# First tile's four merges of a bidirectional delta-rule recurrence: two at a time on two pairs of PSUM banks, with the loads of one direction ordered ahead of the other's

## The reference, cut to what matters

```python
def chunk_gated_delta(q, k, v, g, beta, s0):
    # S_t = a_t (I - b_t k_t k_t^T) S_{t-1} + b_t k_t v_t^T, o_t = S_t^T q_t, in chunks
    a_low = where(strict, einsum('bhnid,bhnjd->bhnij', k * beta, k) * decay, 0)
    sol = triangular_solve(a_low + eye, rhs, lower=True, unit_diagonal=True)
    ...
    def step(S, inp):                      # one chunk after the other
        v_new = u_n - w_n @ S
        o_n = qd_n @ S + att_n @ v_new
        return S * gt_n + kt_n^T @ v_new, o_n
# run once forwards and once backwards over the tokens, 8 heads of 128
```

## Time and profile before

| | |
|---|---|
| three executions | 2710.94 us median, 2702.87 to 2714.01 us |
| the profiled execution | 2701.26 us, of which the span is 2699.5 us |
| mean granted clock of TensorE | 0.932 of full speed |
| TensorE busy | 2307.3 us, 85% of the span |
| VectorE, ScalarE, GpSimd busy | 1019.7, 589.6 and 249.5 us |
| the recurrence's first matmul and the end of its loop | 399.3 and 707.4 us |

### The profile page before, as it was taken

How to read it: one execution, slowest core, us unless ns; L and a number is a source line. 1 busy time by engine, 2 the same in 40 slices (tenths; PEclk the granted TensorE clock), 3 DMA queues, 4 the chain that set the end, 5 groups by cost and what they waited for, 6 DMA issues and landing times. The chain is left out here.

```text
span 2699.5 us, 29938 instructions
## 1 busy us (share of the span) xinstructions
PE 2307.3 (85%) x11804; PEld 1514.6 (56%) x11804; DVE 1019.7 (38%) x1782; ACT 589.6 (22%) x1229; POOL 249.5 (9%) x295
## 2 busy tenths in 40 slices
PE   4999987699785897888888888885998989799998
PEld 2877657589674333333333333333775767688775
DVE  3677526545745010101011010115744554563443
ACT  4442213244411000000000000002332421223311
POOL 4223326500110000000000000000000000000000
PEclk8999988599887999999999999997998999899999
DMA  6123636354410999999999999994220131221030
GB/s 218 58 86 121 215 110 180 82 148 118 152 69 24 417 417 417 417 416 416 417 417 418 417 418 418 416 416 161 90 78 31 32 117 63 100 94 63 32 133 31
DMA packets 209222, 569.87 MB, mean 211 GB/s; under 512 B 62584, under 2 KB 97377, under 8 KB 175713
## 3 DMA queue, kind: packets, MB, share of 16 engines
q1 hardware_dynamic: 202104, 559.45, 54.5%
q0 software_dynamic: 2496, 8.40, 1.0%
q10 hardware_dynamic: 4521, 0.64, 0.1%
HBM read 540.14 MB, written 28.31 MB: 211 GB/s over the span
## 5 line engine op out<-in xcount | busy, mean ns | idle before, releaser
L1897 PE MATMUL ps_gate_up<-expert_ring_early,one_expert_columns 128*64 128x512 f32 x512 | 252.0, 650 | 87.6 <-DMA expert_ring_early<-in_moe_w_up_dram 73.8
L1897 PE MATMUL ps_gate_up<-expert_ring,one_expert_columns 128*64 128x512 f32 x512 | 233.4, 610 | 47.1 <-DMA expert_ring<-in_moe_w_up_dram 47.0
L1964 DVE TENSOR_TENSOR hidden_tokens<-silu_gate,ps_gate_up 64x512 f32<-64x512 f32 x64 | 42.5, 690 | 609.6 <-ACT silu_gate L1943 609.1
L1898 PE MATMUL ps_gate_up<-expert_ring_early,one_expert_columns 128*64 128x512 f32 x512 | 252.8, 651 | 0.0
L1898 PE MATMUL ps_gate_up<-expert_ring,one_expert_columns 128*64 128x512 f32 x512 | 234.0, 611 | 0.0
L1877 PE MATMUL ps_down<-expert_ring,hidden_columns 128*64 128x512 f32 x512 | 226.6, 595 | 0.0
L1878 PE MATMUL ps_down<-expert_ring,hidden_columns 128*64 128x512 f32 x512 | 226.6, 595 | 0.0
L1897 PEld LDWEIGHTS ps_gate_up<-expert_ring_early,one_expert_columns 128*64 128x64 f32 x512 | 73.4, 149 | 249.0 <-issue 249.0
L1897 PEld LDWEIGHTS ps_gate_up<-expert_ring,one_expert_columns 128*64 128x64 f32 x512 | 69.9, 141 | 193.0 <-issue 193.0
L1877 PEld LDWEIGHTS ps_down<-expert_ring,hidden_columns 128*64 128x64 f32 x512 | 67.5, 137 | 130.1 <-issue 127.9
L846 DVE SCALAR_TENSOR_TENSOR conv_out<-conv_in,tap_columns,conv_out 128x770 f32<-128x770 f32 (+1 forms) x96 | 124.2, 1294 | 3.4
(11 more groups left out here) (506 smaller groups left out, 4625.9 us busy)
## 6 DMA issues: line engine op xcount, KB each, us to landing
expert_ring<-in_moe_w_down_dram SPq DMA_DIRECT2D x64, 2048.0 KB, 19.5
expert_ring_early<-in_moe_w_gate_dram SPq DMA_DIRECT2D x32, 2048.0 KB, 16.1
expert_ring_early<-in_moe_w_up_dram SPq DMA_DIRECT2D x32, 2048.0 KB, 20.6
expert_ring<-in_moe_w_gate_dram SPq DMA_DIRECT2D x32, 2048.0 KB, 22.5
expert_ring<-in_moe_w_up_dram SPq DMA_DIRECT2D x32, 2048.0 KB, 24.2
win_ring<-in_gdn_w_in_dram SPq DMA_DIRECT2D x16, 1024.0 KB, 7.9
late_mod_ring<-in_w_mod_dram SPq DMA_DIRECT2D x16, 1024.0 KB, 5.4
stream_raw<-in_w_in_even_dram SPq DMA_DIRECT2D x16, 1024.0 KB, 5.2
```

The source lines that it names most:

```text
L1897: mm(psA[LO, c], xe[:, e, k], gu[s0][:, j, cols], start=(k == 0), stop=(k == KC - 1))
L1898: last = mm(psA[HI, c], xe[:, e, k], gu[s1][:, j, cols], start=(k == 0), stop=(k == KC - 1))
L1964: nc.vector.tensor_tensor(hid[HI, c % 2], sg[HI, c % 2], psA[HI, c], ALU.mult).then_inc(hidden, 1)
```

## The change

Merges 1 and 3 get banks 4 and 5 as their pair, all others keep banks 6 and 7. Merges 0 and 1 are interleaved step by step, then merges 2 and 3, all ahead of the loop, on TensorE and on ScalarE. On VectorE `merged(0)` and `merged(1)` stand behind rows 16 and 17, `merged(2)` and `merged(3)` behind rows 26 and 27. `product32(1)` waits for all decays (the last readers of banks 4 and 5), `product32(2)` and `product32(3)` for `w_ready` of 1 and 2. SyncE stores direction 0's blocks, loads direction 0's inputs, and only then stores and loads direction 1's.

```diff
-        psC, qS, aN, ps32, psX = bank[0:4], bank[4], bank[5], bank[6], bank[7]
+        psC, qS, aN = bank[0:4], bank[4], bank[5]
+        merge_bank = lambda y: (bank[4], bank[5]) if y in (1, 3) else (bank[6], bank[7])
...
                 for d in DIRS:
                     scatter(0, d)
-                for d in DIRS:
                     inputs(0, d)
...
                     pe.wait_ge(in_loaded[d], 16 * IN_DMAS * (g + 1))
-                    if y:
-                        pe.wait_ge(w_ready, y)
+                    if y == 1:
+                        pe.wait_ge(decays, len(PIECES))
+                    elif y:
+                        pe.wait_ge(w_ready, y if y >= 4 else y - 1)
                     for h in range(Q):
-                        last = mm(ps32[:, h], B5[d][:, HEAD[c].start + h], Td[d][:, HEAD[c].start + h], start=True, stop=True)
+                        last = mm(merge_bank(y)[0][:, h], B5[d][:, HEAD[c].start + h], Td[d][:, HEAD[c].start + h], start=True, stop=True)
                     last.then_inc(p5, 1)
...
-                    if g == 0:
-                        return
                     pe.wait_ge(updated, x - 3)
...
-                for y in range(3):
-                    product32(y)
-                    merge32(y)
-                    product64(y)
-                    merge64(y)
-                product32(3)
+                for pair in ((0, 1), (2, 3)):
+                    for part in (product32, merge32, product64, merge64):
+                        for y in pair:
+                            part(y)
                 for g in range(NT):
                     x, y, more = 4 * g, 4 * (g + 1), g + 1 < NT
-                    k_state(x)
-                    merge32(y - 1)
-                    k_state(x + 1)
-                    product64(y - 1)
-                    k_state(x + 2)
-                    merge64(y - 1)
-                    k_state(x + 3)
+                    if g:
+                        k_state(x)
+                        merge32(y - 1)
+                        k_state(x + 1)
+                        product64(y - 1)
+                        k_state(x + 2)
+                        merge64(y - 1)
+                        k_state(x + 3)
                     if more:
                         product32(y)
                     solve(x)
...
-                for y in range(3):
-                    keep32(y)
-                    keep64(y)
-                    fill64(y)
-                keep32(3)
+                for pair in ((0, 1), (2, 3)):
+                    for part in (keep32, keep64, fill64):
+                        for y in pair:
+                            part(y)
                 for g in range(NT):
                     x, y, more = 4 * g, 4 * (g + 1), g + 1 < NT
-                    keep64(y - 1)
-                    fill64(y - 1)
+                    if g:
+                        keep64(y - 1)
+                        fill64(y - 1)
                     scale_k(x)
                     if more:
...
-                MERGED_AFTER = {14: 0, 23: 1, 30: 2}
+                MERGED_AFTER = {16: 0, 17: 1, 26: 2, 27: 3}
...
                 for g in range(NT):
                     x, y, more = 4 * g, 4 * (g + 1), g + 1 < NT
                     remainder(x)
-                    merged(y - 1)
+                    if g:
+                        merged(y - 1)
```

More of the change, by code:

```diff
@@ L1119, in merge32 @@
                     h0, er = HEAD[c].start, EARLY[d]
-                    flat = ps32[er].rearrange("p a b -> p (a b)")
+                    flat = merge_bank(y)[0][er].rearrange("p a b -> p (a b)")
                     pe.wait_ge(e5, y + 1)
@@ L1125, in merge32 @@
                     for h in range(Q):
-                        last = mm(psX[:, h], P5s[y % 2][:, h], Wd[d][:, h0 + h], start=True, stop=True)
+                        last = mm(merge_bank(y)[1][:, h], P5s[y % 2][:, h], Wd[d][:, h0 + h], start=True, stop=True)
                     last.then_inc(x2, 1)
@@ L1131, in product64 @@
                     h0, er, lr = HEAD[c].start, EARLY[d], LATE[d]
-                    flat = ps32[lr].rearrange("p a b -> p (a b)")
+                    flat = merge_bank(y)[0][lr].rearrange("p a b -> p (a b)")
                     pe.wait_ge(t6, y + 1)
@@ L1276, in keep32 @@
                     act.wait_ge(p5, y + 1)
-                    nc.scalar.activation(P5s[y % 2][:, :, :], ps32[:, :, :], ACT.Copy).then_inc(e5, 1)
+                    nc.scalar.activation(P5s[y % 2][:, :, :], merge_bank(y)[0][:, :, :], ACT.Copy).then_inc(e5, 1)
                 def keep64(y):
                     d = (y % 4) // 2
-                    flat = ps32[LATE[d]].rearrange("p a b -> p (a b)")
+                    flat = merge_bank(y)[0][LATE[d]].rearrange("p a b -> p (a b)")
                     act.wait_ge(p6, y + 1)
@@ L1287, in fill64 @@
                     d = c // 2
-                    flat = ps32[EARLY[d]].rearrange("p a b -> p (a b)")
+                    flat = merge_bank(y)[0][EARLY[d]].rearrange("p a b -> p (a b)")
                     act.wait_ge(x26, y + 1)
@@ L1408, in merged @@
                     dve.wait_ge(x2, y + 1)
-                    nc.vector.tensor_tensor(W5[c][:, :, :], Wd[d][:, HEAD[c]], psX[:, :, :], ALU.subtract).then_inc(w5, 1)
+                    nc.vector.tensor_tensor(W5[c][:, :, :], Wd[d][:, HEAD[c]], merge_bank(y)[1][:, :, :], ALU.subtract).then_inc(w5, 1)
                 def remainder(x):
```

## The result

The changed kernel takes 2684.37 us (median of 5 executions, 2680.91 to 2691.79) against 2709.22 us (5 executions of before, three of them those shown above): ratio 0.9925, 95% interval 0.9905 to 0.9945, so 15 to 26 us faster (20 by the ratio; the medians alone lie 24.8 us apart). The profiled execution took 2684.37 us with a span of 2682.6 us, 16.9 us less than the profiled one of before.

What follows compares the result with a forecast made beforehand. The prediction took the four merges ahead of the loop, 41.3 us with gaps at the low clock, as the bound. 2710.94 - 16.0 = 2694.9 us for the median (2685.3 us profiled), range 2684 to 2702.

Steps and rivals of the forecast that it cites:

- Bound: In the recurrence, only the 41.3 us of four TensorE merges had time to give; everything behind them waits for them.
- Loads: SyncE's queue ahead of the merges: direction 0's inputs land earlier, 0.4 us gained; direction 1's last load lands at 495.1.
- The chain of waits: Merges: in pairs, ScalarE waits of 0.69, 0.47 and 0.56 us go, leaving 7.1 us per merge at the low clock.
- The clock's rise: TensorE in the merges: without gaps it reaches 2.4 GHz about 5 us into the first pair (bounds 3.4 us and never).
- rival 1: The clock stays low through the pairs of merges: 13.3 us gained, 2697.6 us; chance 0.20.
- From here VectorE decides.: Second pair: VectorE's rows set its end, `merged(2)` at 505.1, loop at 510.0; TensorE stands some 4 us before `product64(2)`.
- The head of the loop: The loop's first 3.4 us ran at the low clock; 1.7 us gained or up to 1.7 lost, taken as zero.
- The latent inverse: VectorE's last rows and copy end near 512; the store that reads it, at 528, keeps 16 us of cover.
- Rivals 2, 3 and 4: Direction 1's loads waited off later, 2700.9 us (0.16); slower at `product32(2)`, 2730 us (0.04); pairs not overlapping, some 1 us.

Runs made afterwards that it cites:

- after_again: The changed kernel run once more, unaltered: ratio 0.9939 to the kernel before, median 2690.16 us.
- c: The kernel before with only VectorE's table changed, `merged(1)` and `merged(2)` behind rows 18 and 23 in place of 23 and 30: ratio 0.9968.
- a: The changed kernel with SyncE's old order, both directions' stores first, then both directions' loads: ratio 0.9942 to the kernel before.
- d: The changed kernel with `merged(2)` and `merged(3)` behind rows 22 and 23 in place of 26 and 27: ratio 0.9926 to the kernel before.
- e: The changed kernel with SyncE's old order of loads and `merged(2)`, `merged(3)` behind rows 22 and 23: ratio 0.9927 to the kernel before.
- f: The changed kernel with the old order of loads, `merged(2)`, `merged(3)` behind rows 20, 21 and `merged(4)` behind row 26: ratio 0.9912 to the kernel before.
- g: As f, but with the change's order of loads: ratio 0.9921 to the kernel before.
- f_again: f run once more, unaltered, beside the changed kernel on one chip: ratio 0.9921 to the kernel before, median 2683.99 us.
- h2: f with 16 extra matmuls, of no use to the result, on TensorE ahead of the first pair: ratio 0.9894 to the kernel before.

## Why the prediction was right

The forecast was 16.0 us, of which 0.4 in T1 and 15.6 in T2; the profile pair shows 0.57 and 14.74, the repeated medians 16.5. The first medians lie 24.8 us apart, and the ratio beside them says 20 (interval 15 to 26, which holds 16.0); no cause found here accounts for what lies over the 15 us of the traces.

- **Bound.** Right. L and the stages behind moved as a block: L is 181.35 and 181.59 us, and the stages behind it differ by 0.41 us.
- **Loads.** Right in size: 0.4 forecast, 0.57 in the profile pair, 0.5 between the means of T1. Direction 1's last load was forecast 10.8 us behind `product32(0)` and landed at 11.2 (493.12 - 481.88).
- **The chain of waits.** Right in kind, the size 7% too high. A merge without its gaps was put at 7.1 us at the low clock and measured 6.6: in after_again the first pair took 13.3 us, all of it at 0.50 (489.78 to 503.06). One of the three ScalarE waits stayed against the forecast, the 0.56 us of the last `fill64` ahead of the loop. The 5.12 us of merge 1 were the table's (c: 5.2).
- **The clock's rise.** Right in kind, the size not: it came 3.2 us into the first pair for my 5, and 2.9 to 4.3 us into it in a, d, e and both runs of f. In after_again and g it did not rise in the first pair but in the second, some 16.4 us after `product32(0)`. That is rival 1 for half of the way; no run had the low clock through both pairs. Rival 1's price, 13.3 us for T1 and T2, is near what after_again gained in them, 13.9; it lost 2.2 us of it in L, which I had not put to it.
- **"From here VectorE decides."** This held and it was the step that carried the number: `merged(2)` was forecast at 505.1 - 484.3 = 20.8 us behind `product32(0)` and came at 20.7 (502.56 - 481.88); in a, with TensorE 6.43 us too early, it came at 20.8 (507.15 - 486.32) and T2 was the same. That the number fits so well is in part luck, since two errors cancel. Row 18 was forecast at 493.7 - 484.3 = 9.4 us and began at 8.1 (490.00 - 481.88), in the main because the clock rose early; rows 18 to 26 were put at 11.4 us and took 12.6 (490.00 to 502.56), most of the excess in rows 24 to 26, 3.8 us for 2.9 in the kernel before. Why these rows were slower was not tested. Another part failed: I had TensorE wait there for some 4 us at the high clock. In the changed kernel its clock had fallen before the second pair, it was free for `product64(2)` only at 502.99, and the two engines came to the same time by different roads. Had I costed the second pair at the low clock I would have found the same end.
- **The head of the loop.** Taken as zero with 1.7 us either way. It was near zero in the first run (0.24 us lost), 2.2 us lost in after_again, d and e (8.7 to 9.5 us at 0.50), 1.7 gained in f_again (179.69 us). So the bound of 1.7 us lost was too narrow.
- **The latent inverse.** Right: it ended 17.3 us ahead of the store that reads it.
- **Rivals 2, 3 and 4.** None showed in the total. The 1.77 us wait for direction 1 was there, but within VectorE's time, and a without it was no faster. What the forecast did not see is that the clock could fall in this wait, as it did in the changed kernel and in d: with VectorE's rows out of the way (d against e) T1 + T2 was 2.9 us longer with the change's order.

The range, 2684.0 to 2702.0, held the median of 2684.37 us by 0.4 us: that is luck, since the range's lower end was the best case less the spread of single executions. The repeated median, 2690.16, lies well inside it.

## What to carry to other kernels

Where three engines hand one small product round, put a second product in flight before anything else, and then look for the engine that has work of its own in between: here it was VectorE, whose table of row numbers was worth 5 us in the serial kernel for one line (c) and, with the old order of loads and `merged(4)` moved too, 6 us or more in the paired one (f) that the change left lying. An order of loads that gains 0.5 us ahead of a chain can cost more inside it (2.9 us, d against e, by one trace each), which shows only when the slower engine is out of the way. Judge such an edit by stretches between fixed instructions of the trace and not by the total: single executions of one kernel here differ by 10 us and more (the kernel before by 21 us on one chip), in part because the clock rises early, late or not at all in the same stretch, so one profile of after says little on the clock.

## What the runs showed of the hardware

- TensorE's clock did not rise in 16.32 us of work without a gap (after_again), nor in 11.03 us (changed), yet in the changed kernel it rose after 3.22 us of the first pair. In d the loop's head stayed low for 8.37 us without a gap. The Trainium skill (TensorE: Matmul & The Clock Gate, What you observe) has the clock up around 4 us into sustained matmuls; in six of the eight traces with pairs and no extra work it was up 2.9 to 4.3 us into the first pair, near that; in after_again it took four times as long, and the measurement decides.
- The clock fell in a wait, as in a: TensorE stopped at 501.2 and the clock was down from 502.8 us on. The Trainium skill (TensorE: Matmul & The Clock Gate, HAM oscillation) tells of such falls in waits for data; the trace agrees. But how soon it falls differs from run to run: 3.8 us after the stop in the kernel before, 1.6 us in a, 0.6 us in the changed kernel. In h2 it did not fall in a wait of 1.72 us ahead of `product32(0)`, and in f it fell at 496.3 us with TensorE at work, after waits of 0.56 and 0.18 us.
- A VectorE instruction on two SBUF operands stood through a GpSimd copy. In d the last row's product took 1.96 us (0.33 in the changed kernel) beside GpSimd's copy of the inverse, and ended with it; in the kernel before a row stood through it in the same way, 1.96 us from 510.70. VectorE's row, then GpSimd's:

```profile
508.73 1.96 DVE L911 TENSOR_TENSOR row_update<-blocks_lat,inverse_lat 128x31 f32<-128x31 f32 x1
```

```profile
508.68 1.93 POOL L916 COPY blocks_lat<-inverse_lat 128x1024 f32<-128x1024 f32 x1
```

The Trainium skill (SBUF — State Buffer, Who interferes with whom) says that the two engines share a pair of ports, an exclusive lock, and that a VectorE instruction with two SBUF inputs contends with a GpSimd instruction that reads SBUF; the trace agrees, GpSimd ended at 508.68 + 1.93 = 510.61 and VectorE at 508.73 + 1.96 = 510.69 us. In the changed kernel no VectorE row fell on it; there VectorE's own copy began first (508.07 us, 1.14 us long) and GpSimd's took 2.66 us in place of 1.93.
